# A two-layer hybrid decoder step on one core: memory keys and first projection in one block, bias tables built beside other stages, prompt attention by periods, 1088 token columns

## What is computed

```
xn = rmsnorm(x, g_mix[0]);  zp = xn @ w_in_nsa        # the first input projection, 15 tiles of 128 columns
kv = rmsnorm(mem, g_mem[i]) @ w_mem_kv[i]             # memory keys and values, both layers
nsa_kv: k_slc = rmsnorm(k), k_win = rmsnorm(k), kc, vc = compress(rows of 64 tokens)
per query: l_c = q.kc + bias_c   (16 blocks)          -> softmax -> o_c = p_c @ vc
           l_s = q.k_sel + bias_s (all past tokens)   -> softmax -> o_s
           l_w = q.k_win + bias_w (last 512 tokens)   -> softmax -> o_w
           o = g0 * o_c + g1 * o_s + g2 * o_w          # gates: sigmoid of three columns of zp
bias(d) = rel_bias[bucket(d)], constant from distance 128 on
```

## Time and profile before

| | us |
|---|---|
| median of 3 runs | 3249.93 |
| lowest, highest | 3248.84, 3257.4 |
| the profiled execution | 3255.0 |
| its span, first to last instruction | 3253.1 |
| mean granted TensorE clock in it | 0.955 |

### The profile page before, as it was taken

One profiled execution on the slowest core, in us unless ns is written; L12 is line 12 of the kernel. 1 busy time (PEld: TensorE's weight loads), 2 busy tenths in 40 slices (PEclk: granted clock), 3 DMA queues, 4 the chain that ended last, 5 costly groups with the idle time before them and its releaser, 6 DMA issues. The chain is left out here.

```text
span 3253.1 us, 51238 instructions
## 1 busy us (share of the span) xinstructions
PE 3024.3 (93%) x19509; PEld 2777.4 (85%) x19509; DVE 1555.6 (48%) x3312; ACT 817.7 (25%) x1508; POOL 952.2 (29%) x414
## 2 busy tenths in 40 slices
PE   5999967888888998999999999989899999999998
PEld 5999954555556668999999999989799999999998
DVE  4310215666655442575363453558418635626353
ACT  4101004666663331332020110122404301202010
POOL 2340000000000004444444444353134444444443
PEclk7997987999998998999999999999999999999999
DMA  4115622000005642111111111131311111111112
GB/s 156 46 32 188 216 88 107 1 2 1 1 23 187 194 123 107 50 40 42 49 44 40 46 38 53 35 118 37 121 39 57 39 46 46 39 52 36 48 40 84
DMA packets 126987, 220.39 MB, mean 68 GB/s; under 512 B 15946, under 2 KB 90556, under 8 KB 125648
## 3 DMA queue, kind: packets, MB, share of 16 engines
q1 hardware_dynamic: 108400, 201.55, 19.3%
q10 hardware_dynamic: 18432, 16.79, 1.6%
HBM read 202.58 MB, written 19.84 MB: 68 GB/s over the span
## 5 line engine op out<-in xcount | busy, mean ns | idle before, releaser
L394 POOL TENSOR_SCALAR weights_high<-weights_whole 128x1024 fp32r<-128x1024 f32 (+2 forms) x176 | 459.6, 2612 | 1150.8 <-PE banks L429 926.2
L425 PE MATMUL banks<-ffn_in_high,weights_high 128*128 128x364 f32 x2112 | 467.9, 330 | 16.7 <-DVE ffn_in_low L300 9.0
L427 PE MATMUL banks<-ffn_in_low,weights_high 128*128 128x364 f32 x2112 | 468.8, 330 | 0.0
L429 PE MATMUL banks<-ffn_in_high,weights_low 128*128 128x364 f32 x2112 | 468.4, 330 | 0.0
L396 POOL TENSOR_TENSOR weights_low<-weights_whole,weights_high 128x1024 fp32r<-128x1024 f32 (+2 forms) x176 | 385.6, 2191 | 26.1 <-issue 5.9
L425 PEld LDWEIGHTS banks<-ffn_in_high,weights_high 128*128 128x128 f32 x2112 | 368.5, 189 | 18.9 <-issue 18.8
L2598 DVE SCALAR_TENSOR_TENSOR conv_out<-conv_ext,conv_w,conv_out 128x1024 f32<-128x1024 f32 x176 | 320.6, 1822 | 113.3 <-ACT conv_out L2534 98.3
L429 PEld LDWEIGHTS banks<-ffn_in_high,weights_low 128*128 128x128 f32 x2112 | 369.3, 189 | 0.0
L427 PEld LDWEIGHTS banks<-ffn_in_low,weights_high 128*128 128x128 f32 x2112 | 368.5, 189 | 0.0
L2534 ACT ACTIVATE conv_out<-conv_ext,conv_b,conv_w 128x1024 f32<-128x1024 f32 (+1 forms) x176 | 138.3, 835 | 543.9 <-DVEq L2589 543.8
L2626 DVE TENSOR_TENSOR x<-x,banks 128x1092 f32 x64 | 82.7, 1292 | 393.5 <-PE banks L429 393.5
(11 more groups left out here) (388 smaller groups left out, 4687.8 us busy)
## 6 DMA issues: line engine op xcount, KB each, us to landing
weights_whole<-in_w_up SPq DMA_DIRECT2D x88, 512.0 KB, 3.5
past_rows<-in_kv_pages SPq DMA_DIRECT2D x160, 128.0 KB, 2.4
z<-in_kv_pages SPq DMA_DIRECT2D x96, 128.0 KB, 2.5
weights_whole<-in_w_down SPq DMA_DIRECT2D x32, 384.0 KB, 3.1
weights_whole<-in_w_down SPq DMA_DIRECT2D x32, 320.0 KB, 2.9
x<-in_cmp_pages ACTq DMA_DIRECT2D x64, 128.0 KB, 5.7
x<-in_cmp_pages SPq DMA_DIRECT2D x64, 128.0 KB, 5.5
cmp_rows<-in_cmp_pages ACTq DMA_DIRECT2D x64, 128.0 KB, 5.6
```

What stands on the lines that cost most here:

```text
L394: pool.tensor_scalar(high, whole, 1.0, None, ALU.mult)
L425: pe.matmul(o, wh, high[:, at], start=kk == 0, stop=False)
L427: pe.matmul(o, wh, low[:, at], start=False, stop=False)
L429: last = pe.matmul(o, wl, high[:, at], start=False, stop=kk == len(terms) - 1)
```

## The change

The diff does five things:

1. `first_stage` takes the place of `memory_kv`, the loading of constants and `project_normed`. It is one block. The memory weights of the two layers share one buffer `mem_weights`, so that the second layer's are loaded only when the first layer's are split. The parts of layer 0 lie where the token parts `in0_high` and `in0_low` come later, those of layer 1 in the upper part of `z`. ACT and DVE go on to the tokens when the products of layer 0 are scaled. The row of biases is made here too, and ACT stores it, once for each of 128 partitions, to DRAM (2.4 MB).
2. The attention constants, the sigmoid and transposition of the gates, the transposed values and the table of near biases move into `front`. The near biases are now read from DRAM already in the wanted order, without PE. The edge and block tables are built by POOL at the start of `prompt_attention`; the sample tables by DVE at its end.
3. `prompt_attention` works in 24 periods of two units, a small one (t = x) and a large one (t = 7 - x). The scores of a period come in 6 phases, each of at most 512 columns for each of two heads, into three banks in rotation; a phase waits only until DVE has taken the second last bank. The phases of period p + 2 are spread evenly over the transposition groups of period p. DVE runs the phases with the two `weigh` of a period between them; three banks instead of two hold transpositions.
4. All projections multiply 1088 instead of 1092 columns: the third cut has 360. DVE then takes a product with two instructions (2 cuts, and the third) where it took it with one.
5. `rest_of_pairs` and the padding columns are filled in to match.

```diff
+def with_banks(k, s, *aps):
+    split = (CUTS - 1) * CUT
+    full = [ap[:, 0:split].rearrange("p (b n) -> p b n", n=CUT) for ap in aps]
+    return ((*full, cut_set(k, s)[:, 0:CUTS - 1, :]),
+            (*(ap[:, split:TE] for ap in aps), cut_set(k, s)[:, CUTS - 1, 0:TE - split]))
...
-            cuts = [(out[:, cut, :], slice(cut * CUT, (cut + 1) * CUT)) for cut in range(CUTS)]
+            cuts = [(out[:, cut, 0:min(CUT, TE - cut * CUT)], slice(cut * CUT, min((cut + 1) * CUT, TE))) for cut in range(CUTS)]
...
+    # first_stage, SP
+        for h in range(2):
+            sp.wait_ge(w_split[h], 1)
+            sp.dma_start(mem_w[:, half(h), :], k.ins["w_mem"][1][:, half(h), :]).then_inc(w_loaded[2 + h], 16)
+        for s in range(2):
+            w.load(sp, s, s, w_src[s], cols)
...
+    # first_stage, PE
+        for i in range(KC):
+            if i == KC - 2:
+                key_sums(0)
+                pe.wait_ge(tables_loaded, 16 * len(TABLES))
+                pe.matmul(row_bank, c["relx"], c["onehot"], start=True, stop=True).then_inc(row_ready, 1)
+            products(1, i)
+        pe.wait_ge(keys_rooted, 1)
+        pe.wait_ge(row_copied, 1)
+
+        def multiply(m, j, s):
+            ready = (lambda i: tokens.wait_chunk(pe, i)) if isinstance(m, int) and m == 0 else None
+            pe.wait_ge(taken, m + 1)
+            w.multiply(pe, m, s, terms, cut_set(k, s), ready)
+            if isinstance(m, int) and m == 0:
+                key_sums(1)
...
+    # first_stage, ACT, between the token chunks and their squares
+            if i == KC - 2:
+                root_keys(0)
+                act.wait_ge(row_copied, 1)
+                act.dma_start(bass.AP(k.row_dram.tensor, 0, [[RW, H], [H * RW, P], [1, RW]]), ...).then_inc(k.row_stored, 16)
+            if i == KC - 1:
+                square_keys(1)
+            if i == KC + 1:
+                root_keys(1)
...
+    # first_stage, DVE
+        scale(0)
+        dve.wait_ge(w_split[1], 2)
+        def between(i):
+            if i == KC - 3:
+                dve.wait_ge(row_ready, 1)
+                dve.tensor_copy(row[:, :], row_bank).then_inc(row_copied, 1)
+            if i == KC - 1:
+                scale(1)
+                finish(0)
+        tokens.dve(dve, between)
...
+    # front: SP at its end; ACT at its start
+            sp.wait_ge(hidden, B)
+            load_near_bias(k, sp, near_loaded)
+            act.activation(z[:, Z_GATE, :], z[:, Z_GATE, :], ACT.Sigmoid).then_inc(gates_on, 1)
...
+    # prompt_attention, PE
+            def score(p, f):
+                at = p * PHASES + f
+                if at >= 1:
+                    pe.wait_ge(taken, G * at - 1)
+                t, keys = ((large, [(Z_KW, first, first + CUTW)]), (small, [(Z_KS, 0, (small + 1) * P)]),
+                           (small, [(Z_KW, 0, (small + 1) * P)]), (large, [(Z_KS, 0, wl - 512)]),
+                           (large, [(Z_KS, wl - 512, wl)]), (large, [(Z_KW, first + CUTW, first + WK)]))[f]
...
+            for j in range(-1, NB):
+                if j >= 0:
+                    for p, f in places.get(2 * j, ()):
+                        score(p, f)
+                turn(2 * j + 2)
+                turn(2 * j + 3)
+                if j >= 0:
+                    for p, f in places.get(2 * j + 1, ()):
+                        score(p, f)
+                    values(2 * j)
+                    values(2 * j + 1)
...
+    # prompt_attention, DVE
+            for p in range(NP):
+                for f in range(PHASES):
+                    if p + 2 < NP:
+                        phase(p + 2, f)
+                    if p + 1 < NP and f in (1, 3):
+                        weigh(2 * p + 2 + f // 2)
```

1105 lines of the change are left out of this document (580 added, 525 removed).

## The result

| | before | after |
|---|---|---|
| median, us | 3251.61 (4 runs) | 3138.95 (4 runs, 3136.93 to 3141.62) |
| ratio | | 0.9652, 95% interval 0.9640 to 0.9664 |
| profiled execution's span, us | 3253.1 | 3137.4 |
| mean granted TensorE clock | 0.955 | 0.964 |

The changed kernel is 3.5% faster, 112.7 us by the medians where 106 were forecast. The page of the changed kernel, part 1, answers to the earlier trace rows: 55 us less of TensorE's busy time (which counts overlapping matmuls), and the rest of the gain is time in which it had stood still.

A forecast was written before the change was run, and what follows sets the result against it. TensorE was taken to bound the FFN, busy throughout, and to stand still in three places elsewhere. Gains of 26 + 33 + 40 + 7 = 106 us gave 3144 us from 3249.9, range 3092 to 3192.

The forecast's parts named there:

- The three idle places: TensorE stands still before the first projection tile, between `front` and the first attention scores, and in the attention waiting for DVE.
- Part 1: First stage, memory products to third projection tile: overlapping memory and token work gains 26 us, bounds 18 and 28.
- the risk I had named: First stage: layer 1's second half of weights, sharing one buffer, is split at 39.9 us, against 40.3 when TensorE wants it.
- Part 2: End of `front` to first biased score: tables, gates and values made beside `front` gain 33 us, between 27 and 36.
- Part 3: Attention: working in periods with spread phases gains 40 us, between 0 and 115; a head pair takes 67.8 instead of 75.1.
- Other loss: Attention, per head pair: lower clock and short gaps beyond TensorE's work and its waits fall from 9.9 to 6 us.
- Part 4: All projections: 1088 columns instead of 1092 save four columns in each of 4104 matmuls, 7 us gained.
- The waits only move: Attention: DVE's `weigh` sits between phases and the attention stays at 468 us; 3184 us in all, chance 0.16.
- the first stage doesn't overlap: First stage: with one weight buffer the memory products end late, gaining 0 instead of 26; 3170 us, chance 0.04.
- TensorE becomes the bound: Attention: little but TensorE's own work remains, some 95 us gained; 3089 us in all, chance 0.15.
- The clock falls more often: Attention: short pauses hold half the work at the lower clock, 90 us more than now; 3274 us, or 3229, chance 0.06.
- Lock step: Attention: DVE and TensorE wait for each other's whole queue, 26.0 instead of 18.8 us a period; 3357 us, chance 0.03.

The follow-up runs named there:

- the experiment above: Two banks instead of three hold transpositions in the attention, against the changed kernel: 3140.35 us, ratio 0.9642 to the kernel before, attention 409.8 us.

## Why the prediction was right, and where its terms were off

**What bounds the kernel.** The three idle places were the right ones, and the stage table shows each of them shorter. The fourth part, which needed no idle place, was also right in itself.

**Part 1, 26 forecast, 22.8 measured.** The mechanism held: DVE takes the third tile at 93.86 instead of 115.3. Three steps of the working were short. The timeline of DVE after, with the six low parts:

```profile
36.49 13.51 DVE L280 SCALAR_TENSOR_TENSOR in_low<-x,g_mix,in_high 128x1092 fp32r<-128x1092 f32 x6 [3.23 <-POOL mem_weights_low L599]
49.93 0.54 DVE L766 COPY bias_row<-banks 12x384 f32<-12x384 f32 x1
```

They took 2.25 us each and not 1.74, because POOL parts weights from 36.50 to 48.85 beside nearly all of them (two of the six took 3.46 and 3.43 us); in the kernel before POOL began 3 us after DVE. They began 1.4 us earlier than assumed, though, so the copy ended only 1.6 us late. The second step was TensorE's pause. I had it end its products at 47.5 and stand still for 1.5 us. It ended them at 45.3, stood still until 50.57, and then ran its first products at the lower clock level (1.24 us for three, as in the earlier trace rows), which the sum had no term for; the tile ended at 64.4 and not 61.0. The third: the additions behind ACT's root at 65.47 took 10.3 us for six, not 8.2, since one of them took 3.3 us beside POOL, and ended at 77.6 instead of 72. The second-layer weights, the risk I had named, were in time. Moving one wait gave back 5 us, which shows the second of these as the largest. The single trace is also on the slow side for this stage: the mean of eight executions is 237.1.

**Part 2, 33 forecast, 32.3 measured.** Term by term it nearly holds. `front` grew by 6 us (195.2 to 201.2; forecast 4.9), and from its end to the first biased score there are 6.8 us, as forecast. The POOL timeline shows the term made up differently:

```profile
441.65 0.42 POOL L1233 MEMSET sion_weights_then_tables<- 128x384 f32 x1 [94.71 <-issue]
442.21 2.77 POOL L1235 TENSOR_TENSOR sion_weights_then_tables<-sion_weights_then_tables,edge_mask 128x1536 f32<-128x1536 f32 x1
```

POOL starts 2.4 us after the block does, where I had taken 0.6 for the block's start and 1 for clearing semaphores, and adds in 2.77 us instead of 3.7. No row shows that it is the clearing that takes this time.

**Part 3, 40 forecast, 61.8 measured.** The mechanism was right and two terms were too large. Four head pairs take 781.55 - 523.21 = 258.3 us (timeline of ACT, before), 64.6 each where 67.8 were forecast.

```profile
523.21 0.21 ACT L1466 ACTIVATE logits_blocks<-logits_blocks 128x32 f32<-128x32 f32 x1
...
781.55 0.21 ACT L1466 ACTIVATE logits_blocks<-logits_blocks 128x32 f32<-128x32 f32 x1
```

Waits are 3.9 us of a pair instead of 6. (The 9.4 that I started from was a mean with the attention's start in it; in the four pairs of the earlier trace rows the kernel before waits 21.5 + 11.2 us for DVE, 8.2 a pair.) I had let two phases in six wait; in the steady part only the last of a period does. That the whole attention's waits come to 36.0 us, just as forecast, is a coincidence: 16.2 of them lie before 500 us, in the start, and 5.4 of these are one wait until POOL's tables of part 2 are there. "Other loss" is 64.6 - 55.8 - 3.9 = 4.9 and not 6. The two terms give (2.1 + 1.1) x 6 = 19 of the missing 22 us. The rest, 2.5, is the start, where I had added 4. How the gain is made up can be read from windows over four pairs, before and after (length, PE busy first, clock third from the end):

```profile
591.50:891.80 300.30, 263.39 (x2340) 168.04 (x2338) 191.36 (x1005) 184.71 (x489) 0.00 (x0) 0.97 0.01 1
```

```profile
523.21:781.55 258.34, 242.20 (x2290) 165.82 (x2290) 195.75 (x1068) 182.38 (x489) 0.00 (x0) 0.99 0.01 2
```

Of 42.0 us, 20.8 are less idle time (36.9 to 16.1) and 21.2 are less busy time for the same products. The clock rose from 0.97 to 0.99, and matmuls cost less each: 283 instead of 295 ns in the mean for those with the values.

It would be tempting to say that fewer pauses paid for both. The same four pairs in three of the experiments show otherwise (windows of the kernel that waits for both heads, and of the one with the bias row's wait moved, whose attention is the changed kernel's):

```profile
530.14:812.21 282.07, 246.66 (x2290) 167.58 (x2290) 196.05 (x1068) 182.54 (x489) 0.00 (x0) 0.98 0.01 1
```

```profile
517.83:774.65 256.82, 240.64 (x2290) 164.66 (x2290) 195.89 (x1068) 182.39 (x489) 0.00 (x0) 1.00 0.01 2
```

| four head pairs, us | length | idle | busy | clock |
|---|---|---|---|---|
| before | 300.3 | 36.9 | 263.4 | 0.97 |
| changed | 258.3 | 16.1 | 242.2 | 0.99 |
| changed, bias row moved | 256.8 | 16.2 | 240.6 | 1.00 |
| changed, waits for both heads | 282.1 | 35.4 | 246.7 | 0.98 |
| changed, phases in pairs | 348.2 | 76.1 | 272.1 | 0.90 |

With both heads TensorE stands still as long as in the kernel before, and its busy time is still 17 us less. Among the changed kernels busy time follows the clock. An estimate from the rows: a mean share of 0.97 over 300.3 us costs at most 9.0 us against full speed, 0.99 over 258.3 costs 2.6, so the clock makes some 6 of the 21 us (up to 9, as the shares are rounded). The other 12 to 15 belong to what all changed kernels have in common and the kernel before has not: the order of transpositions and products in twos of groups, and scores in fewer, wider matmuls (386 instead of 432 in these pairs). The third bank of transpositions is not it, by the experiment above. Which of the others it is stays open. So the step that was mis-sized is the one that let "a part of the other loss go", 9.9 to 6: it went to 4.9, and pauses were the smaller part of the reason.

**Part 4, 7 forecast.** Measured at 7 us by putting the columns back (2292.7 against 2285.5). But the stages behind the attention were 1.1 us longer, since the padding rule of change 5 put a wait before POOL's weights in layer 1. I had read item 5 as filling in and costed it at nothing, without following POOL's queue behind it; the kernels without that wait have 4.5 us less. Another 2 to 4 us are missing between the one execution of the kernel before and the mean of those after, and stay open. A candidate, not tested, is the clock: 0.98 in this stage before, 0.97 in the changed kernel.

**The rivals.** "The waits only move" and "the first stage doesn't overlap" did not happen. "TensorE becomes the bound" was nearly half true: idle time in the steady part is 6% of it. "The clock falls more often" did not happen in the changed kernel, but happened with phases in pairs. The case in the Trainium skill's page "TensorE: Matmul & The Clock Gate", section "A second HAM failure mode: psum-queue depth-cycling", comes from a kernel whose clock went up and down because TensorE was idle briefly and often while it cycled through banks. It is not borne out for the changed kernel, whose scores and transpositions rotate over three banks each at 0.99. With phases in pairs the clock did fall, to 0.90, with pauses of up to 4.3 us; the cycling through banks was the same in both, so here the length and number of the pauses decide. "Lock step" did not hold for a period. It did hold for the start, where 6.7 us lay, more of it work at the lower clock level than waiting.

## What to carry to other kernels

Where one engine makes work that another must take before a buffer is free, the place of the pieces can be worth more than their number: here six places per period, with nothing else changed, decide 117 us in 407. When such a wait grows, follow it past the engine that it names: here that one was itself waiting for a third. A wait that a change adds "for tidiness" (eight padding columns, a copy of a row) costs what stands behind it in its queue, so each new wait is to be followed along its queue, and put as late as what it protects allows. At the start of such a rotation the later users of the buffers are not there yet; lend theirs to the first pieces.

## What the runs showed of the hardware

- Long pauses are paid twice. With 117.8 us of waits for DVE, up to 4.3 us each in the steady part, the granted clock there was 0.90, and four head pairs cost TensorE 272.1 us of busy time instead of 242.2. With 66.8 us of waits, none over 2.3 us in the steady part, the clock in the 260 us window stayed at 0.99.
- One DVE instruction with two inputs from SBUF takes 1.33 us alone and up to 3.46 us while POOL works; six in a row beside a busy POOL took 13.51 us. The Trainium skill's page "SBUF — State Buffer", section "🔬 SBUF: two separate sides", says that such an instruction and one of POOL that reads SBUF exclude each other for their whole length. The trace agrees for POOL's subtractions with two inputs: the DVE instructions that began at 39.88, 46.58 and 68.73 ended at 43.34, 50.01 and 72.05, each 1.15 to 1.16 us after the subtraction beside it (42.19, 48.85, 70.90). It does not agree for POOL's rounding with one input, from 42.16 to 45.97: one DVE instruction from 43.27 to 45.39 lay wholly inside it, by the rows, and took 2.12 us.
- Between 440 and 460 us, where the attention starts, the granted clock was 0.50 in the kernels with three banks at the start, 0.65 and 0.73 in the two with six.
- POOL's first work in the attention block came 2.4 us after the block began (441.65 against 439.27 on TensorE), with nothing before it that a row shows; with the tables moved to `front` it is 2.4 us again (442.98 against 440.61).
